# A two-block kernel: row squares and a weight cut moved at one seam, two input transfers split, part of a product on another engine

## What is computed

```python
def reference(x, ...):
    x = first_block(x, ...)
    return second_block(x, mem_2, ...)

def first_block(x, ...):
    h = rmsnorm(x, g_mix)                                  # the first norm
    a_x, a_gate, hy, gates = split(h @ w_in)
    y_a = (rg_lru(conv(a_x)) * gelu(a_gate)) @ w_a_out     # forward and backward scan
    v, x1, x2 = split(conv(hy))
    z = v
    for n, gate in enumerate((x1, x2)):                    # two long convolutions, by spectra
        z = gate * fftconv(z, k[n], filt_bias[n])          # irfft(U * K)
    y_b = z @ w_b_out
    x = x + (g_a * y_a + g_b * y_b) @ w_o
    h = rmsnorm(x, g_ffn)
    vals, idx = top_k(softmax(h @ w_router).T, 32)         # 16 experts take 32 tokens each
    x = x.at[idx].add(vals * ((silu(h[idx] @ w_gate) * (h[idx] @ w_up)) @ w_down))
    return rmsnorm(x, g_final)

def second_block(x, mem, ...):
    for l in range(2):
        x = x + 0.5 * swiglu(rms_norm(x, norm_ffn1[l]))    # ffn1
        x = x + concat(rwkv7_mixer, chunk_attention, multiscale_pool)(rms_norm(x)) @ w_out[l]
        x = x + memory_cross_attention(rms_norm(x), rms_norm(mem))
        x = x + 0.5 * swiglu(rms_norm(x, norm_ffn2[l]))    # ffn2
    return x
```

## Time and profile before

| | us |
|---|---|
| median of 3 runs | 2585.06 |
| lowest and highest | 2584.26, 2587.38 |
| the profiled execution | 2582.32 |
| its span | 2580.4 |
| TensorE busy | 2292.9 (89%) |
| VectorE busy | 1070.6 (41%) |
| ScalarE busy | 855.1 (33%) |
| GpSimd busy | 79.5 (3%) |

### The profile page before, as it was taken

The page is one execution under the profiler, slowest core; times in us unless marked ns, Lnnn a source line. Parts: engine busy times, 40 slices in busy tenths (PEclk is TensorE's granted clock), DMA queues, the critical chain, the costliest instruction groups (busy, mean ns, idle before and its releaser), DMA issues.

```text
span 2580.4 us, 37341 instructions
## 1 busy us (share of the span) xinstructions
PE 2292.9 (89%) x15324; PEld 1634.5 (63%) x15324; DVE 1070.6 (41%) x1681; ACT 855.1 (33%) x1348; POOL 79.5 (3%) x87
## 2 busy tenths in 40 slices
PE   7999998777777777777779999999999999999999
PEld 7996593233333322233237889788888889878887
DVE  7868860000000000000015557756455547666554
ACT  4483141001000100000015445545445445545543
POOL 0000012000000000000000000100000000200000
PEclk9999999878888888888889999999999999999999
DMA  6534089999999999999996544043556554123553
GB/s 245 179 131 152 4 356 405 427 427 427 428 427 427 427 427 427 427 428 426 427 387 204 195 165 170 19 169 126 194 182 207 193 184 167 67 101 130 181 194 114
DMA packets 116822, 669.21 MB, mean 259 GB/s; under 512 B 10826, under 2 KB 14069, under 8 KB 56400
## 3 DMA queue, kind: packets, MB, share of 16 engines
q1 hardware_dynamic: 111376, 650.14, 64.7%
q0 software_dynamic: 3008, 12.96, 1.4%
q10 hardware_dynamic: 2304, 4.20, 0.4%
HBM read 662.01 MB, written 5.24 MB: 259 GB/s over the span
## 4 chain that ended last, share of the span: by engine, by line
PE 59%; DMA 25%; DVE 4%; SPq 4%; issue 3%; ACT 2%; DVEq 1%; POOLq 1%; POOL 0%; ACTq 0%
PE psd L698 22%; PE psd L692 10%; PE psx L698 9%; DMA hx<-in_w_down 7%; DMA ring<-in_w_down 7%; DMA scr<-in_w_up 7%; SPq L3229 4%; PE psx L1131 2%; PE psd L1114 2%; PE psd L1072 1%; PE psx L1386 1%; PE psd L1062 1%; DMA e_w_lo<-in_w_up 1%; DMA e_w_hi<-in_w_up 1%; PE psx L942 1%
## 5 line engine op out<-in xcount | busy, mean ns | idle before, releaser
L2238 DVE TENSOR_TENSOR w_lo<-ring,w_hi 128x1024 fp32r<-128x1024 f32 x436 | 515.6, 1220 | 391.0 <-ACT w_hi L1661 389.7
L1661 ACT ACTIVATE w_hi<-ring 128x1024 fp32r<-128x1024 f32 x436 | 437.2, 1048 | 479.4 <-PE psd L698 253.7
L698 PE MATMUL psd<-w_hi,h_cut 128*128 128x512 f32 x1536 | 481.5, 395 | 5.9 <-DVE w_lo L2238 2.3
L692 PE MATMUL psd<-h_cut,w_hi 128*128 128x256 f32 x1824 | 336.0, 286 | 12.0 <-DVE h_cut L2238 7.8
L698 PEld LDWEIGHTS psd<-w_hi,h_cut 128*128 128x128 f32 x1536 | 284.2, 188 | 63.9 <-DVE w_lo L2238 2.7
L698 PE MATMUL psd<-w_lo,h_cut 128*128 128x512 f32 x768 | 300.5, 391 | 0.0
L692 PEld LDWEIGHTS psd<-h_cut,w_hi 128*128 128x128 f32 x1824 | 286.8, 194 | 16.9 <-issue 14.2
L692 PE MATMUL psd<-h_cut,w_lo 128*128 128x256 f32 x912 | 259.5, 285 | 0.0
L1650 ACT ACTIVATE scr<-psd 128x512 f32<-128x512 f32 (+1 forms) x54 | 30.9, 573 | 566.7 <-PE psd L1088 359.2
L698 PE MATMUL psx<-w_hi,halves 128*128 128x512 f32 x704 | 218.0, 391 | 0.0
L2238 DVE TENSOR_TENSOR scr<-psd,scr 128x512 f32<-128x512 f32 (+1 forms) x24 | 15.9, 668 | 437.6 <-PE psd L1072 436.3
(11 more groups left out here) (416 smaller groups left out, 2900.6 us busy)
## 6 DMA issues: line engine op xcount, KB each, us to landing
ring<-in_ffn_wi SPq DMA_DIRECT2D x88, 1024.0 KB, 5.7
scr<-in_w_gate SPq DMA_DIRECT2D x48, 1024.0 KB, 26.6
scr<-in_w_down SPq DMA_DIRECT2D x48, 1024.0 KB, 26.2
scr<-in_w_up SPq DMA_DIRECT2D x48, 1024.0 KB, 26.7
ring<-in_ffn_wo SPq DMA_DIRECT2D x44, 1024.0 KB, 4.9
ring<-in_w_gate SPq DMA_DIRECT2D x32, 1024.0 KB, 26.8
ring<-in_w_up SPq DMA_DIRECT2D x32, 1024.0 KB, 27.0
ring<-in_w_down SPq DMA_DIRECT2D x32, 1024.0 KB, 26.5
```

Source lines behind the costliest of these rows:

```text
L692: mm = pe.matmul(o, w[u], a[:, v, :], start=start and i == 0, stop=stop and i == 2, **kw)
L698: mm = pe.matmul(o, a[:, u, :], w[v], start=start and i == 0, stop=stop and i == 2)
L1661: act.activation(hi, src, ACT.Copy).then_inc(hi_cut, 1)
L2238: return dve.tensor_tensor(o, a, b, op)
```

## The change

Four things are changed.

1. Start. The order of the constants' columns changes so that the first 258 (identity, ones and the two epsilons) are enough for the first norm. These are issued first, then x in two transfers of half its size, the parameters, weight slot 0, and then the other 1382 columns (`con_rest`). VectorE writes `seam_eps` first of all, and ScalarE takes the root of it before x is there. ScalarE squares each half of x as it lands, cuts only the first half of slot 0 ahead of the norm's root, and the second behind it. PE makes 6 matmuls of 128 columns into a bank that is not used ahead of the norm's sums and 12 behind them (`keep_clock`).
2. Spectra. In each of the four halves the subtract and the add of group f = 0 go from VectorE to GpSimd (`cross`). VectorE waits for them before the folds. The products f0 and f1 of the two groups lie in different places (`cross_of`).
3. Seam behind the experts, ScalarE and VectorE. The four row squares, which stood one behind the other after the last scaled piece, go between the other steps. The third slot of ffn1 is cut ahead of the roots on ScalarE, and ahead of the row scales on VectorE.
4. Seam, PE. The turn of piece 0 goes between the third and the fourth block of the last expert's sum.

The core of the diff:

```diff
-            act.wait_ge(S("x_in"), 16)
-            norm("g_mix", between=first_slot, mid=lambda: prime(cutter, ("a_x", 0)))
+            act.wait_ge(S("tiny_set"), 1)
+            act.activation(seam[:, 20:21], seam_eps, ACT.Sqrt)
+            norm("g_mix", each=lambda i: act.wait_ge(S(f"x_in{i // 2}"), 16), between=lambda: cutter.upto(0, 0),
+                 before_cut=lambda: cutter.upto(0), mid=lambda: prime(cutter, ("a_x", 0)))
+            act.wait_ge(S("con_rest"), 16)
...
-            pe.wait_ge(S("par_in"), 16)
+            def keep_clock(bank, n):
+                for _ in range(n):
+                    pe.matmul(bank[:, 0:P], ident, ones, start=True, stop=True)
             pe.wait_ge(S("con_in"), 16)
+            keep_clock(psd[0], 6)
             norm("g_mix")
+            keep_clock(psd[0], 12)
+            pe.wait_ge(S("con_rest"), 16)
...
                         read(tt_(f1, ui[:, :], kr, ALU.mult))
-                        dve.drain()
-                        tt_(yr, yr, f0, ALU.subtract)
-                        tt_(yi, yi, f1, ALU.add)
-                        dve.drain()
+                        if f == 0:
+                            dve.drain().then_inc(S("cross"), 1)
+                        else:
+                            dve.drain()
+                            tt_(yr, yr, f0, ALU.subtract)
+                            tt_(yi, yi, f1, ALU.add)
+                            dve.drain()
+                    dve.wait_ge(S("cross_summed"), 2 * n + half + 1)
...
+            def cross(n, half):
+                pool.wait_ge(S("cross"), 2 * n + half + 1)
+                f0, f1 = cross_of[0]
+                pool.tensor_tensor(spec_y[:, 0, :], spec_y[:, 0, :], f0, ALU.subtract)
+                pool.tensor_tensor(spec_y[:, 2, :], spec_y[:, 2, :], f1, ALU.add)
+                pool.drain().then_inc(S("cross_summed"), 1)
...
                 for b in range(4):
+                    if last and b == 3:
+                        turn_piece("norm_ffn10", "moe_acc", 0, 0)
...
-            for i in range(2):
-                turn_piece("norm_ffn10", "moe_acc", 0, i)
+            turn_piece("norm_ffn10", "moe_acc", 0, 1)
```

More of the change, by code:

```diff
@@ L2447, in ffn @@
                         evict(i)
+            dve.memset(seam_eps, EPS * EPS).then_inc(S("tiny_set"), 1)
+            for i in range(2):
+                dve.wait_ge(S(f"x_in{i}"), 16)
+            for i in (0, 4):
+                dve.wait_ge(sq_ready, i // 2 + 2)
+                tt_(sq[:, i:i + 2, :], sq[:, i:i + 2, :], sq[:, i + 2:i + 4, :], ALU.add).then_inc(S("first_sums"), 1)
             dve.wait_ge(S("par_in"), 16)
-            dve.wait_ge(S("con_in"), 16)
             lam = par[:, PCOL["lru_lambda"]:PCOL["lru_lambda"] + 16]
@@ L2781, in from_moe @@
                 row_sums_made(g)
+                cutter.upto(SN[("ffn1", 0, "gu", 1), 0])
                 row_scales(g)
@@ L3212, in slot @@
                 sp.dma_start(ring[n % RING][:, 0:words], src).then_inc(land[n % RING], 16)
[L3214 to L3215 removed]
+            early = CCOL["bones"]
+            sp.dma_start(con[:, 0:early], A["consts"][:, 0:early]).then_inc(S("con_in"), 16)
+            for i in range(2):
+                sp.dma_start(x[:, 4 * i:4 * i + 4, :], A["xT"].rearrange("(k p) t -> p k t", p=P)[:, 4 * i:4 * i + 4, :]).then_inc(
+                    S(f"x_in{i}"), 16)
             sp.dma_start(par[:, :], A["params"]).then_inc(S("par_in"), 16)
```

27 lines of the change are left out of this document (13 added, 14 removed).

## The result

The changed kernel takes 2569.99 us (median of 6 runs, 2569.3 to 2573.52); the kernel before, run beside it, takes 2585.74 us (6 runs, 2584.24 to 2587.38). The ratio is 0.9945, 95% interval 0.9935 to 0.9954: between 11.9 and 16.8 us less, best estimate 14.2. The forecast was 9.5 us less, 2575.6, with a range from 2573.0 to 2582.0. The sign was right, the size was too small, and the range missed the time.

What follows compares the result with a forecast made beforehand. PE was taken to bound the kernel before and behind the experts, the weights' stream within them. Start 3.5, spectra 1.1 and seam 4.9 sum to 9.5 us, from 2585.06 to 2575.6 us; range 2573.0 to 2582.0.

Steps and rivals of the forecast that it cites:

- Part 1, the chain: Start: slot 0 lands at about 9.5 us and the reciprocal starts at 11.9 instead of 15.05, 3.15 us gained.
- Part 1, the clock: Start: with idle matmuls before it, a_x begins at the fast rate, clock 1.00; 0.6 us, taken as 0.35.
- Part 2, the spectra: Last half: GpSimd takes one group's subtract and add, so the folds end at 312.7 instead of 313.8: 1.1 us.
- The lead through the experts: Experts: w_down's first issue moves with the first expert, to near 384 us, so the earlier gain passes in full.
- rivals 3 and 4: Experts' stream: start's and spectra's lead lost, 2580.2 us (chance 0.10); or 1.6% lower stream rate, 2590.5 us (chance 0.05).
- The sum: Whole kernel: start 3.5, spectra 1.1 and seam 4.9 add up to 9.5 us less.
- Part 3, the seam: Behind the experts: first wait 1.1, third slot's wait 2.3, clock 1.6, less 0.1 coming back: 4.9 us.
- rival 1: Seam: a wait stays because scaled copies come late, and the clock drops as before; 2578.7 us, chance 0.18.
- late next: Seam, after the third slot: VectorE's product comes at 1369.4 us, PE asks at 1369.3, so 0.1 us comes back.
- The clock's 1.6 us: Seam, behind the third slot's wait: 24 matmuls take 5.6 instead of 7.2 us if no long wait is left.
- The base: Whole kernel: the gain, worked out from one execution of 2582.3 us, is taken from the runs' median of 2585.06.
- the forecast's high ends: Whole kernel: the most favourable ends of start, spectra and seam together give 10.8 us less.

Runs made afterwards that it cites:

- seam alone: The kernel before with only the seam's changes (turn of piece 0, squares spread out, third slot cut ahead of the roots): 2577.36 us, ratio 0.9965.
- seam without the turn: The kernel before with the seam's squares spread out and third slot cut earlier, but piece 0's turn left in its old place: one execution, 2585.24 us.
- before_pad: The kernel before with 18 narrow idle matmuls, nine ahead of each of the last two experts: 2583.71 us, ratio 1.0.
- seam_clock: The kernel before with eight idle matmuls in TensorE's wait for the third slot of ffn1: 2588.01 us, ratio 1.0015.

## Why the prediction was right about the parts and wrong about the sum

Stage by stage. "Pair" is the difference of the two first traces; "all traces" sets the mean of the traces that have a stage as before against the mean of the four with the whole change in it (the changed kernel twice, the two with more idle matmuls). For ffn1 to the turn it is the six and the eight of above, for the experts' two rows the five with the old start and spectra and no idle matmuls there.

| stage | forecast | pair | all traces |
|---|---|---|---|
| start of a_x | 3.15 | 3.18 | 3.1 |
| a_x to the wait of 2.0 us (the start's clock) | 0.35 | 0.28 | 0.5 |
| that wait to the last inverse (the spectra) | 1.1 | 2.47 | 2.0 |
| last inverse to w_down's issue | 0 | -1.43 | 0.2 |
| w_down's issue to the last expert's sum | 0 | 1.35 | 1.3 |
| to ffn1's first matmul | 1.1 | 1.22 | 1.2 |
| ffn1 to the first turn (2.3 + 1.6 - 0.1) | 3.8 | 4.27 | 4.5 |
| behind the turn | 0 | -2.14 | -0.4 |
| sum | 9.5 | 9.2 | 12.4 |

- **Part 1, the chain: right.** Slot 0, the reciprocal and a_x came where they were put (11.87 for 11.9, 16.13 for 16.15). The rule on the fixed cost of a transfer (the Trainium skill, "DMA: Bandwidth & Descriptors", Anatomy of one DMA), taken serially, would have put slot 0 at 13.5, an estimate; the trace has it at 9.64, so what is fixed in a transfer overlaps here. The page gives its figure for transfers that GpSimd issues, and these are SyncE's.
- **Part 1, the clock: right in size, wrong in what was to show it.** The forecast took 0.35 us and asked for clock 1.00 at a_x's start. It was 1.00 only until about 17 us, then 0.57 to 21 (PE stands for 2.63 us once the idle matmuls, at the fast rate, are done; the forecast had reckoned them slow and lasting until 16.1). Both traces of the changed kernel are 0.35 us below the mean of the six old ones from a_x to the wait of 2.0 us (187.07 against 187.42). Without the dip it is 0.7 (186.72).
- **Part 2, the spectra: mechanism right, 1.4 us for 1.1.** GpSimd's operations took 1.27 us each and VectorE's none longer. The wait went from 2.17 to 1.67 us. That is what the prediction's own numbers give (PE 0.6 us earlier, the folds 1.1 earlier); the wait of 1.1 us that it names under "What will show it" doesn't follow from them. These waits account for 1.1 us, and 0.3 aren't placed. The rule on the shared port (the Trainium skill, "SBUF — State Buffer", SBUF: two separate sides) wasn't put to the test here: GpSimd's two end at 303.22 us, 0.9 us before VectorE's next operation with both inputs in SBUF (304.13).
- **The lead through the experts: right.** w_down was issued at 384.08 us, 4.50 before 388.58, and from there to the landing of the last expert weight it is 951.7 to 952.0 us in all 14 traces: rivals 3 and 4 are out.
- **The sum: the step that failed.** It has the clock in two places (0.35 and 1.6 us) and puts it at nothing in all others, and it has no term for the issue stop. Behind the wait of 2.0 us a dip costs 1.1 us; the six old traces all have it, the changed kernel has it in one of two. In the last expert, behind TensorE's last wait for weights (it ends at 1320.68 us before and 1316.48 after), the clock from 1320 to 1330 us is 0.66 before and 1.00 after. From the landing of the last weight to the last sum it is 5.1 to 6.1 us in the four traces with the clock low for longest there (before, seam alone, seam without the turn, before_pad) and 3.0 to 3.8 in the ten others. That is the 1.3 us of the table. In the pair it is hidden by chance, as the changed kernel's first execution lost 1.43 us to a longer dip ahead of the experts (granted clock 0.53 from 369 to 376 us). Whether the change itself makes these dips rarer or 14 traces show it by luck stays open. The issue stop of 1.2 to 1.5 us is gone in both traces of the changed kernel, but behind the turn more dips outweigh it (-0.4).
- **Part 3, the seam: mechanism right, two terms mis-sized.** 1.22 for 1.1, and no wait for the third slot: rival 1 is out. Without dips ffn1 to the turn went from 20.04 to 17.42 us, so the wait with what comes back gave 2.6, not 2.2, though "late next" was 0.6 us and not 0.1. The clock's 1.6 us were taken from one execution as if they were the wait's fixed price; with the waits there are 0, 1 or 2 dips of 1.65 us, 7 in six traces, and none in the eight without the third slot's wait, so it is worth 1.9 on average.
- **The base: not what failed, but luck in the pair.** The sum was made from one execution and taken from the median of others. That execution was a quick one: its last stage takes 1206.01 us, the least of all 14 traces (up to 1211.38), because it has no dip there. Less the dips (1.7 us each) and the issue stops that each trace shows in it, this stage takes 1203.3 to 1205.5 us in all 14. So the 9.2 us of the pair are near the forecast by luck. The median as base did no harm: less 12.4 instead of 9.5 it gives 2572.7.

12.4 us by the traces, 13.2 ± 0.5 by all the runs and 14.2 by the first are above even the forecast's high ends (10.8), so a range that took them with a microsecond of spread ended at 2573.0, 3.0 above the measured median. Of the 2.9 us between 9.5 and 12.4, 1.5 lie in the experts' rows, 0.9 between the wait of 2.0 us and the last inverse (0.3 the spectra, 0.5 the dip), 0.8 in the seam and 0.1 in the start, less 0.4 behind the turn. Open are what makes a dip come or stay away, the price of the issue stop in the times, some 3 of the 4.5 us that the kernel without idle matmuls lost, and of seam_clock's 3.2 ± 0.7 us (by the means) the 1.9 beyond its second issue stop (1.2 to 1.5 us). The dips were never held still: no kernel was found that has none.

## What to carry over

Before a term is taken from one trace, lay two or three executions of the same kernel side by side and mark what comes and goes. Price a wait as its length plus the dips that follow it on average, and do so for every wait whose place or length the change moves, not only for the one that it removes. A gain that a run seems to put down to one stage should be cut by one more mark: here 1.7 us "of the start's clock" were 0.7 of it and 1.0 of a dip 190 us later. When instructions are added to an engine only to fill time, look far behind them too: they shift where the engine's issue stops fall, and a gain or loss of a microsecond or two can be theirs.

## What the runs showed of the hardware

- The granted clock falls to its lower level (1.2 of 2.4 GHz) for a few microseconds, at different places in different executions of one kernel. Such a dip costs 1.7 us where PE is the bound (0.57 and 0.58 over 4 us, in the kernel before's second execution) and 1.1 us behind the wait at 203 us (105.81 against 104.75 us). The runs of the kernel before scatter over 8 us (2580.94 to 2588.87, 75 runs); of the 5.1 us between its two traces, two dips make 3.4.
- TensorE stops for 1.2 to 1.5 us at a fixed place in its program, where many small matmuls follow each other, with no wait in the profile; 18 matmuls inserted hundreds of microseconds earlier remove it, 8 shift it by about 8 and bring a second one. In each of the nine stops a 16 KB packet of the DMA queue of kind "instruction" starts 2.3 to 2.8 us before its end.
- The weights' stream takes 951.7 to 952.0 us from the first w_down's issue to the last landing in all 14 traces, whenever it starts (383.2 to 391.6 us).
- The clock's column can read 1.00 at the very start while matmuls run at the slow rate. In the changed kernel without idle matmuls the first row of a_x takes 0.77 us, as in the earlier trace rows, and this stretch reads

```profile
16.00:19.00 3.00, 2.80 (x13) 2.83 (x14) 3.00 (x7) 0.74 (x2) 0.00 (x0) 1.00 0.59 249
```

There the length of a matmul tells the rate, not the column.
